# One 512-column matmul for the high and low activations of a split-precision product, with readers that add two halves of a PSUM bank

## The reference

```python
# first block
p = h @ w_l
y_a = (attn * jax.nn.silu(z_a)) @ w_pa
y_b = (_fourier_mix(u_b) * jax.nn.silu(z_b)) @ w_pb
return (g_a * y_a + g_b * y_b) @ w_o
# second block
proj = u @ w_in[l].astype(f32)
merged = (jax.nn.sigmoid(gate_a) * (o_a @ p_a[l].astype(f32))
          + jax.nn.sigmoid(gate_b) * (o_b @ p_b[l].astype(f32)))
h = h + gate1 * (merged @ w_out[l].astype(f32))
ff = jax.nn.silu(u @ w_gate[l].astype(f32)) * (u @ w_up[l].astype(f32))
h = h + gate2 * (ff @ w_down[l].astype(f32))
```

## Time and profile before

| | before |
|---|---|
| median of 3 runs | 2976.53 us (2974.68 to 2979.34) |
| span of the profiled execution | 2980.7 us |
| PE busy | 2920.2 us, 98% of the span |
| DVE busy | 2010.6 us, 67% |
| ACT busy | 1413.5 us, 47% |
| POOL busy | 395.7 us, 13% |
| read from HBM | 612 MB, 207 GB/s over the span |

### The profile page before, as it was taken

The page is one execution under the profiler, slowest core; times in us unless marked ns, Lnnn a source line. Parts: engine busy times, 40 slices in busy tenths (PEclk is TensorE's granted clock), DMA queues, the critical chain, the costliest instruction groups (busy, mean ns, idle before and its releaser), DMA issues. The chain is left out here.

```text
span 2980.7 us, 56517 instructions
## 1 busy us (share of the span) xinstructions
PE 2920.2 (98%) x23016; PEld 2808.0 (94%) x23016; DVE 2010.6 (67%) x3126; ACT 1413.5 (47%) x2150; POOL 395.7 (13%) x1052
## 2 busy tenths in 40 slices
PE   7899999999999999999999999999999999999999
PEld 4479999999989989999999999999989999999999
DVE  7867776777777767766677676677877754455544
ACT  5644443444455556555565543343444443344433
POOL 3403310000002332332332310000000000000000
PEclk9999999999999999999999999999999999999999
DMA  8855567778846535444545458778768756655554
GB/s 280 275 176 203 205 218 238 276 257 286 288 156 204 165 131 166 163 163 148 171 151 167 164 185 282 268 254 289 260 208 272 253 188 182 186 181 185 183 186 141
DMA packets 196246, 622.43 MB, mean 209 GB/s; under 512 B 20224, under 2 KB 38416, under 8 KB 195216
## 3 DMA queue, kind: packets, MB, share of 16 engines
q1 hardware_dynamic: 195984, 618.81, 62.0%
HBM read 612.43 MB, written 4.21 MB: 207 GB/s over the span
## 5 line engine op out<-in xcount | busy, mean ns | idle before, releaser
L259 PE MATMUL ps<-act_lo,whi 128*128 128x256 f32 (+1 forms) x6416 | 1647.6, 291 | 10.2 <-DVE act_lo L255 9.2
L259 PE MATMUL ps<-act_hi,whi 128*128 128x256 f32 (+1 forms) x6416 | 1613.7, 286 | 0.0
L245 DVE TENSOR_TENSOR wlo<-raw,whi 128x1024 fp32r<-128x1024 f32 (+3 forms) x946 | 1128.2, 1214 | 499.8 <-ACT whi L236 270.8
L259 PEld LDWEIGHTS ps<-act_lo,whi 128*128 128x128 f32 x6416 | 1231.8, 192 | 22.8 <-ACT act_hi L236 9.9
L259 PEld LDWEIGHTS ps<-act_hi,whi 128*128 128x128 f32 x6416 | 1233.3, 192 | 9.8 <-issue 3.8
L236 ACT ACTIVATE whi<-raw 128x1024 fp32r<-128x1024 f32 (+3 forms) x946 | 936.7, 1027 | 186.5 <-PE ps L259 184.6
L259 PE MATMUL ps<-act_hi,wlo 128*128 128x256 f32 (+1 forms) x6416 | 988.2, 288 | 3.6 <-DVE wlo L245 2.7
L259 PEld LDWEIGHTS ps<-act_hi,wlo 128*128 128x128 f32 x6416 | 854.5, 192 | 17.2 <-issue 5.8
L236 ACT ACTIVATE t<-ps 128x256 f32<-128x256 f32 (+4 forms) x298 | 112.0, 378 | 504.8 <-PE ps L259 488.7
L255 DVE SCALAR_TENSOR_TENSOR acc<-raw,c_act,acc 128x1024 f32<-128x1024 f32 x210 | 267.9, 1278 | 0.0
L245 POOL TENSOR_TENSOR small<-small 128x2 f32<-128x2 f32 (+1 forms) x444 | 152.9, 344 | 301.2 <-ACT t L236 174.4
(11 more groups left out here) (215 smaller groups left out, 2254.0 us busy)
## 6 DMA issues: line engine op xcount, KB each, us to landing
raw<-in_w SPq DMA_DIRECT2D x429, 512.0 KB, 4.8
raw<-in_w_mod SPq DMA_DIRECT2D x192, 512.0 KB, 5.4
raw<-in_w_ada SPq DMA_DIRECT2D x96, 512.0 KB, 5.5
raw<-in_w_gate SPq DMA_DIRECT2D x88, 512.0 KB, 4.5
raw<-in_w_up SPq DMA_DIRECT2D x88, 512.0 KB, 4.7
raw<-in_w_out SPq DMA_DIRECT2D x64, 512.0 KB, 5.4
raw<-in_w_down SPq DMA_DIRECT2D x64, 448.0 KB, 3.8
raw<-in_p_a SPq DMA_DIRECT2D x32, 512.0 KB, 6.1
```

The source lines that it names most:

```text
L245: return (q or DV).put(lambda e: e.tensor_tensor(o, a, b, op), needs, cost=(0.15 if q else 0.09) + size(o) * (0.0021 if q else 0.00104))
L259: return PE.put(lambda e: e.matmul(o, w, x, start=start, stop=stop), needs, tell, cost)
```

## The change

High and low activations now lie in one buffer (`HL`, `MHL`, `FHL`), so that both can be named as one operand of 2 x 256 columns. For a unit of width 256, `mm_hi` issues one matmul of high weights with both, which writes the high part into columns 0 to 255 of the bank and the low part into columns 256 to 511. `mm_lo` adds low weights by high activations into columns 256 to 511. Units of width 512 and `ba_pe` stay as they were. Every reader of such a bank has to add the two halves: most do it through `join`, an ACT copy of the first half into a `t1` tile and a DVE addition of the second, after which the bank is given back and the job goes on with the tile. `add_scaled` does two scaled additions on DVE where there was one. `conv_job` keeps its ACT copy and adds the other half on DVE. The modelled cost of a matmul of the fast type is changed too.

```diff
     def mm(o, w, x, start, stop, needs=(), tell=False):
-        cost = 2 * max(0.107, size(o) / 1200) if x.dtype == F32 else max(0.107, size(o) / 2400) + 0.003
+        cost = 2 * max(0.107, size(o) / 1200) if x.dtype == F32 else max(0.12, size(o) / 2265)
...
+    def mm_hi(u, w, rhs, first, needs):
+
+        x, xh, xl = rhs
+        if u.width == 512:
+            mm(u.out, w, xl, first, False, needs)
+            mm(u.out, w, xh, False, False)
+        else:
+            mm(both(u.bank[:, :]), w, x, first, False, needs)
+
+    def mm_lo(u, w, rhs, last, needs, tell):
+
+        o = u.out if u.width == 512 else u.bank[:, 256:512]
+        return mm(o, w, rhs[1], False, last, needs, tell=tell)
+
+    def join(bank, tok):
+
+        x, f = yield from t1.take()
+        c = copy(x[:, :], bank[:, 0:256], tok + f)
+        yield c
+        a = tt(x[:, :], x[:, :], bank[:, 256:512], ALU.add, c)
+        banks.give(bank, a)
+        return x, a
...
     def silu_job(key, bank, tok):
 
+        x, a = yield from join(bank, tok)
         w, f = yield from t1.take()
-        a = act(w[:, 0:256], bank[:, 0:256], ACT.Tanh, tok + f, scale=0.5)
-        a = stt(w[:, 0:256], w[:, 0:256], 1.0, bank[:, 0:256], ALU.add, ALU.mult, a)
-        banks.give(bank, a)
-        gate_tile[key] = w, a
+        a = act(w[:, :], x[:, :], ACT.Tanh, a + f, scale=0.5)
+        a = stt(x[:, :], w[:, :], 1.0, x[:, :], ALU.add, ALU.mult, a)
+        t1.give(w, a)
+        gate_tile[key] = x, a
...
+    def add_scaled(o, bank, g, x, needs):
+
+        t = stt(o, bank[:, 256:512], g, x, ALU.mult, ALU.add, needs)
+        return stt(o, bank[:, 0:256], g, o, ALU.mult, ALU.add, t)
...
         c = copy(xp[:, 4:260], bank[:, 0:256], tok + f)
-        banks.give(bank, c)
         y, f = yield from t1.take()
         tap = lambda j: col(C_CONV + 4 * (16 * x + h) + j)
         yield c
+        c = tt(xp[:, 4:260], xp[:, 4:260], bank[:, 256:512], ALU.add, c)
+        banks.give(bank, c)
```

More of the change, by code:

```diff
@@ L859, in fourier_job @@
     def fourier_job(g, bank, tok):
-        u, f = yield from t1.take()
-        c = copy(u[:, 0:256], bank[:, 0:256], tok + f)
-        banks.give(bank, c)
+        u, c = yield from join(bank, tok)
         yield c
@@ L892, in tanh_job @@
     def tanh_job(key, bank, tok):
-        w, f = yield from t1.take()
-        a = act(w[:, 0:256], bank[:, 0:256], ACT.Tanh, tok + f, scale=0.5)
-        banks.give(bank, a)
-        gate_tile[key] = w, a
+        w, a = yield from join(bank, tok)
+        gate_tile[key] = w, act(w[:, :], w[:, :], ACT.Tanh, a, scale=0.5)
     def gated_job(key, bank, tok, done):
+        x, t = yield from join(bank, tok)
         while key not in gate_tile:
@@ L903, in gated_job @@
         w, a = gate_tile.pop(key)
-        a = stt(w[:, 0:256], w[:, 0:256], 1.0, bank[:, 0:256], ALU.add, ALU.mult, tok + a)
-        banks.give(bank, a)
-        done(w, a)
+        a = stt(x[:, :], w[:, :], 1.0, x[:, :], ALU.add, ALU.mult, t + a)
+        t1.give(w, a)
+        done(x, a)
     def merge1_a(n):
@@ L1203, in sb_k @@
     def sb_k(h, bank, tok):
+        kg, a = yield from join(bank, tok)
         sq, f = yield from t1.take()
-        kg, f2 = yield from t1.take()
-        s = act(sq[:, :], bank[:, 0:256], ACT.Square, tok + f)
-        c = copy(kg[:, :], bank[:, 0:256], f2, scale=col(C_KN))
-        banks.give(bank, c)
+        s = act(sq[:, :], kg[:, :], ACT.Square, a + f)
+        c = copy(kg[:, :], kg[:, :], s, scale=col(C_KN))
         yield s
@@ L1223, in sb_v @@
     def sb_v(h, bank, tok):
-        vt, f = yield from t1.take()
-        c = copy(vt[:, :], bank[:, 0:256], tok + f)
-        banks.give(bank, c)
+        vt, c = yield from join(bank, tok)
         yield c
@@ L1592, in pa_job @@
             yield None
-            free = [f for x, f in store.left if x is item]
-        a = stt(MA[:, n, :], w[:, :], 1.0, bank[:, 0:256], ALU.add, ALU.mult, tok + a + free[0])
-        banks.give(bank, a)
+            free = [f for y, f in store.left if y is item]
+        a = stt(MA[:, n, :], w[:, :], 1.0, x[:, :], ALU.add, ALU.mult, t + a + free[0])
+        t1.give(x, a)
         t1.give(w, a)
```

109 lines of the change are left out of this document (54 added, 55 removed).

## The result

The changed kernel takes 2985.38 us (median of 5 runs, 2984.36 to 2990.12) against 2976.88 us for the kernel before, run on the same chip: a ratio of 1.0033, 95% interval 1.002 to 1.0045. The forecast was 2897 us with a range of 2880 to 2940, so it failed on the sign as well as on the size. The profiled execution spans 2983.2 us (2980.7 before).

The account below looks back on a forecast made before the run. The prediction took PE's weight matmuls, their number times their pitch, to bound the kernel. From the profiled span, 2980.7 - 84 + 2 - 6 + 9 = 2901.7 us, less 4.2 for the runs' median: 2897 us, range 2880 to 2940.

Parts of the forecast that it names:

- What bounds the kernel: Whole span: time is the number of PE's weight matmuls times their pitch, with some 5% around it.
- What the change removes: 6720 weight tiles on PE: two matmuls instead of three, 0.0125 us saved each, 84 us in all.
- What the readers add: Units of width 256: DVE gets 182 us more, ACT some 112, both hidden under PE, costed at nothing.
- Stage changes and the end: First block's output, both norm boundaries and the tail: one more scaled addition of 0.48 us each, +2 us.
- The heads: Transposes ending the heads: longer matmul cover for POOL's chain nearly removes PE's wait, -6 us, between 0 and -13.
- The planner's clock: Some 430 stretches of small matmuls: jobs' results lose planned slack and come late, +9 us, from 0 to 43.
- Transfers: Heaviest stage: same bytes in less time, 269 GB/s becoming 279, costed at nothing.
- Rival 3: Gates, projections, feed-forward: DVE's queue, standing for ACT's copy in `join`, becomes the bound; 89 us lost, 2986 us, chance 0.05.
- Rival 1: Jobs' results come late in small amounts, PE waiting for `t` tiles between 1050 and 1750 us; 2937 us, chance 0.17.

Follow-up runs that it names:

- e1: The changed kernel with the readers of the kernel before, which read only half of each bank, so results are incomplete: 2936.76 us (0.9858).
- e6: The changed kernel with one more yield in `join`, after the DVE addition: 2956.02 us (0.9924).
- e9: e6 with the planner's old cost of a matmul: 2936.88 us (0.9864).
- e4: The kernel before with the planner's new cost of a matmul and nothing else: 3000.19 us (1.0072).
- e5: e1 with the planner's old cost of a matmul, results incomplete too: 2913.38 us (0.9778).
- e3: The changed kernel with the planner's old cost of a matmul: 2981.71 us (1.0009).
- e12: The kernel before with the planner's new matmul cost and its ACT, DVE and POOL costs raised to near the trace's durations: 2967.13 us (0.9967).
- e16: e1 with the planner's ACT, DVE and POOL costs raised to near the trace's durations, results incomplete: 2903.78 us (0.9756).
- e7: The kernel before, old matmul cost, with wide matmul, joins and changed readers in the feed-forward's units alone (120 of 424): 2958.97 us (0.9934).
- e10: e9 with the same kind of waiting point in further jobs, such as the feed-forward: 2940.01 us (0.9875).
- e8: The changed kernel with each tile's high and low part side by side, so the 512 columns lie in one run: 2986.97 us (1.0023).

## Why the prediction was wrong, step by step

**What bounds the kernel:** right in the main. PE's weight matmuls set the time, with waits on top. But what stands around them is not some 5%: intervals behind small matmuls are 371.5 us and the rest 104.9, together 16% of 2980.7. And PE's waits were not only the single events that the text names. Those make 22.0 us of 57.5; 18.1 us in 20 times for `wlo` and one wait of 9.1 for a `t` tile were left out. Of that, 26.0 us stand in the first 200 us, and the change left them there (25.1).

**What the change removes, 84 us:** right in kind, too large. Measured in the dense stretch it is 0.3595 - 0.3490 = 0.0105 us a tile, 6720 x 0.0105 = 70 us, and 63 to 67 us between whole kernels. The low matmul has 0.119 rather than 0.120, and the wide one took 0.230 where a single group of eight before the change gave 0.2275. A mean from one group with two decimals at its ends was the weak point. The 2.5 ns of the Trainium skill, "TensorE: Matmul & The Clock Gate", section "Back-to-back issue gap", would have given 17 us. The section gives them for an isolated matmul; in this stream, with as many weight loads as matmuls (16296 each), they do not hold, since 63 to 67 us were measured with nothing but the products changed.

**What the readers add, costed at nothing:** this is the step that failed. The work came as counted (DVE 2172.6 us busy against 2010.6, which is 162 of the 182 forecast; ACT 1503.5 against 1413.5, 90 of 112), and DVE stood at 80% where 83% was forecast. But a share of busy time says nothing of what waits behind what. Costed by load they were free; measured they cost 49 us (e1), 68 on the old cost. 29 of these, or 45 on the old cost, went with one waiting point (e6, e9). They were not load, since the point takes no work away: they came from the order, with ACT's queue standing behind a step whose operand was one DVE addition away. The other 19 to 24 us stay open.

**Stage changes and the end, +2 us:** right at the end, too small at the stage changes. The tail has one more reader's step of 0.48 us (the earlier trace rows has its first alone):

```profile
2980.03 0.48 DVE L254 SCALAR_TENSOR_TENSOR t<-ps,mod,h_res 128x256 f32<-128x256 f32 x1 [6.68 <-PE ps L258]
2980.54 0.48 DVE L254 SCALAR_TENSOR_TENSOR t<-ps,mod,t 128x256 f32<-128x256 f32 x1
```

The waits for the second parts of activations went from 9.2 us in 2 times to 18.1 in 5 (14.0 in 3 for those of line 254, 4.1 in 2 for those of line 244), where 1.4 us had been set for three stage changes. What made the new ones is open.

**The heads, -6 us:** right. The transposes' waits for ACT's `t` went from 10.5 us in 7 times to 5.3 in 2; with their other rows (2.9 us for `tx` before, 3.0 for a `t` of DVE's after) the sum is 13.4 before and 8.3 after, 5 us less.

**The planner's clock, +9 us (0 to 43):** the sign and the bounds held, the size did not: 22 us in the kernel before (e4), 23 with the wide matmul (e5 to e1). In the changed kernel as it stands it is 4 us (e3), since the joins without a point hid the rest; with the old cost the kernel was still slower than forecast by 85 us, so this term is not where the forecast failed. The reason given (ACT's and DVE's steps are planned too short beside a matmul priced right) is the one that e12 and e16 bear out.

**Transfers, nothing:** right; 264 GB/s where 269 stood, and PE's list of waits has no DMA in it.

**The rivals.** Rival 3 had price and sign: 2986 us, against 2985.38, from wlo and whi that come late between 475 and 850 because one queue stands for the other. That agreement is partly luck, since it put the loss on DVE standing for ACT's copy, in the gates and the feed-forward, and priced 89 us against a gain of 84. What stood was ACT for DVE's addition, one step further on, and the feed-forward lost nothing (e7). Its test was the right one, "PE waiting for `wlo` or `whi` between 475 and 850": in that window the wait for `whi` went from 2.7 us in 2 times to 7.9 in 8, and 1.9 for `wlo` came new. More of it stood outside that window, 11.5 us for `whi` between 850 and 1050. Against it the text set that the job yields between copy and addition. It does; it does not yield behind the addition, and what is issued there the forecast left out. Rival 1's small waits for `t` tiles between 1050 and 1750 us did not come: the list has one of 3.0 and three below 1 us there, and the 5.3 of the transposes come after 1750. With waiting point and old cost, e9, the kernel lands in the predicted range, at 2936.9, but that is another kernel than the one forecast.

## What to carry to other kernels

When an edit puts one more step on another engine into a chain, look at what is queued behind the first instruction that needs its result, and not only at the busy shares: an engine that is 50% busy and in order still starves its neighbour while the head of its queue waits. A waiting point in the planner behind such a crossing was worth 9 to 76 us at the join, and further points nothing (e10), so try it where the new wait is. Change a modelled cost only together with those that stand beside it. Test the parts of an edit by themselves, since here a gain of 65 us, a loss of 49 and a loss of 22 hid in a difference of 0.3%.

## What the runs showed of the hardware

A wait of 3 us costs more than 3 us. PE in the changed kernel, and its windows of 10 us:

```profile
979.25 3.41 PE L258 MATMUL ps<-act,whi 128*128 128x512 f32 x8 [3.01 <-ACT whi L235]
982.50 1.11 PE L258 MATMUL ps<-act,wlo 128*128 128x256 f32 x8
```

```profile
960.00:970.00 10.00, 10.00 (x64) 8.84 (x62) 9.35 (x19) 5.01 (x9) 6.09 (x15) 1.00 0.62 206
970.00:980.00 10.00, 6.99 (x40) 6.01 (x39) 2.81 (x5) 7.64 (x13) 0.00 (x0) 0.93 0.30 99
980.00:990.00 10.00, 10.00 (x51) 8.30 (x50) 8.48 (x15) 4.19 (x7) 0.00 (x0) 0.90 0.66 211
```

After PE stood 3.01 us, eight wide matmuls take from 979.25 to 982.50, 3.25 us, where eight of the same form took 1.84 at 220.06. The granted clock reads 0.93 and 0.90 in these windows and 1.00 before: for a part of them it was at 1.2 instead of 2.4 GHz, and that wait cost 3.01 + 1.41 us. (It is the longest wait for `whi`. Just before it ACT did not stand: it worked without a pause from 973.63 us on, 1.28 us of it on the loading of a function table at 976.07.) Over the span the mean granted clock of the profiled execution fell from 0.989 to 0.984, which is 2 x 0.005 x 2980 = 30 us more at the lower level, or at most some 15 us of time lost, estimated from half the speed. It is less as far as PE waits in that time: the executions of the kernel before have mean clocks from 0.989 to 0.994, and all of them lie between 2974.7 and 2983.3 us. The wide matmul, at 0.230 us, pays 0.017 us beyond 512 columns at 2.4 GHz (0.2133), the narrow one 0.012. It makes no difference that could be measured whether the wide one's operand is one run of 512 columns (e8) or two of 256 that lie apart.
